# A two-block transformer on one core: norm roots kept 128 tokens wide, and modulation products packed whole between attention units

## The chip, the core and the metric

One core of a Trainium2 chip. The metric is the device time of one launch in microseconds, the median over the runs. All data and all matmuls are fp32. TensorE's clock is granted at one of two levels, 1.2 or 2.4 GHz; the profile shows it as 0.5 or 1.0 of full speed.

## What is computed

A sequence of 512 tokens of width 1024 passes two blocks. The first is a mixture of dilated causal attention (8 heads of 64), a short gated convolution and a cross-attention to 256 memory tokens, followed by an MLP of width 4096. The second adds latent attention and a gated linear recurrence (8 heads), both under a modulation by a condition vector, and a mixture of 32 experts (4 per token). Every part is framed by this norm:

```python
def rms_norm(x, g):
    y = x * lax.rsqrt(jnp.mean(x * x, axis=-1, keepdims=True) + EPS)
    return y * g
...
h = rms_norm(x, g_pre_mix);  proj = h @ w_in            # q, k, v, conv gates b, c, u, and qx
y_attn = dilated_mixture_attention(rope(q), rope(k), v)
y_conv = b * causal_conv3(c * u, conv_w)
y_x    = cross_attention(qx, rms_norm(mem, g_mem) @ w_mem_kv)
y = concat(rms_norm(y_attn), rms_norm(y_conv), rms_norm(y_x)) @ w_out
x = x + rms_norm(y);   x = x + rms_norm(relu(rms_norm(x) @ w_up)**2 @ w_down)
...
mod = silu([c, c_ctx]) @ w_mod + b_mod                  # 1024 x 6144, used from the second block on
```

## The kernel before

Activations lie feature-major: 128 features on the partitions, the 512 tokens (256 for memory and context) along the free dimension, so a 1024-wide row is eight chunks of 128x512. The five engines run their own instruction streams, written out by hand in one order each, and meet in semaphores.

**Weights.** `WT` (from `weight_tiles`, L69) lists all weight tiles of up to 1 MB in the order of use. SP loads them one after the other into a ring of five slots (L630 to L636): tile t waits until the last product pair that uses tile t-5 is complete (`s_pair`). A "pair" is a group of products that fills PSUM banks and is then evacuated by ScalarE (L1198). A w_mod set is a pair of its own kind (`quads`, L450 to L454): four tiles side by side, 32 products whose 32 stationary columns (the conditions) go to four column groups of the array and so to the four 32-partition strips of one bank, taken in turn (L779 to L789).

**First block.** After the pre_mix and mem norms the q, k, v products run (`in1`). Then come 48 attention units, each a head and a block of 128 queries: 32 of the dilated attention (`U_X` = 32, one to four key blocks) and 16 of the memory attention (two key blocks). In `attention` (L869) TensorE issues the scores of unit u+1, a first portion of side products, the transposes of the probabilities of u, a second portion, and the sum of values of u. VectorE does maxima and scaling, ScalarE exponentials and copies. So each unit has two slots for side products, and a list of weights per slot (`UNIT32`, `UNIT16`, `filled` L534) says how many products go where: the rest of w_in and the memory's keys and values (`side1`, 96 products) beside the dilated units, the six modulation sets (`mod`, 192 products, six in each slot) beside the memory units. Between the two runs of units VectorE does the convolution (L1551 to L1559). ScalarE follows the same lists to evacuate (L1227).

**Norms.** There are 23. `norm_stats` (L1454) squares a chunk on VectorE into one of two buffers `sq`; TensorE's `norm` (L823) multiplies it by a 128x128 matrix of ones, which sums over the partitions and repeats the sum on all 128 of them, and accumulates the chunks in `PT`. VectorE then scales and adds EPS (L1465), ScalarE takes the root (L1214), VectorE the reciprocal (L1467), all 128x512, and the chunks are multiplied by gain and `rstd` (`norm_apply` L1472, `add_normed` L1578, `modulated` L1601, `merge` L1642).

**Heads.** In the recurrence (L989 to L1041) the products of head n+1 fill 19 slots of head n (`HEAD_SLOTS`). At its end stand the last slot (`fill(18)`, eight products), the norm of the head's output, and the wait for the evacuation of the next head's products; then slot 0 of the next head with 26 products.

## Time and profile before

| | us |
|---|---|
| median of 3 runs (lowest to highest) | 3635.74 (3634.92 to 3641.96) |
| the profiled execution | 3640.03 |
| its span, first to last instruction | 3638.3 |
| TensorE busy, mean granted clock | 3082.0, 0.908 |
| VectorE busy / ScalarE busy | 1067.0 / 656.8 |
| first-block attention units (148 to 413 us) | 265.4 |
| expert stage (from about 2406 us) | some 1170 |

The rows further down come from the page of this execution and from views of its trace. In a table of stretches the columns are the stretch, its length, then busy time and number of instructions of TensorE (PE), its weight loads (PEld), VectorE (DVE), ScalarE (ACT) and GpSimd (POOL), the granted clock, and the share and rate of DMA. In a list in order of time the columns are start, duration (from first to last of the merged instructions), engine, line, operation, output and inputs with shapes, count, and in brackets how long the engine was idle before and what ended it. In the chain of waits they are start, length, what. Groups of instructions give count, busy time in all, and the mean of one in ns. An fp32 product appears as two MATMUL records.

### The profile page before, as it was taken

Reading aid. Unit: us, or ns where it says so; the run is one execution under the profiler, and the core shown is the slowest. Engines: PE = TensorE matmul, PEld = TensorE weight load, DVE = VectorE, ACT = ScalarE, POOL = GpSimd, SP = SyncE. Lnnn points to the kernel's source line nnn. Section 1 sums busy time; section 2 is a strip of 40 time slices with the busy share of each in tenths; the row PEclk is TensorE's granted clock in tenths of the full one; section 3 lists DMA queues with packets and bytes.
Section 4 is the critical chain, followed back from the end, with each engine's and each line's share of the span. In section 5 each row is a group of like instructions: output and inputs, shape, how many; then the busy total and the mean of one; then the engine's idle time right before and its main releaser. Section 6 shows DMA issues by size and latency. Waiting matters only on the chain.

```text
span 3638.3 us, 44181 instructions
## 1 busy us (share of the span) xinstructions
PE 3082.0 (85%) x18888; PEld 1555.5 (43%) x18888; DVE 1067.0 (29%) x1997; ACT 656.8 (18%) x1344; POOL 193.9 (5%) x180
## 2 busy tenths in 40 slices
PE   6896579999967999899999958458899999899873
PEld 3552234444423666566666644323333333333321
DVE  3342331000042221455555552511111111111115
ACT  1131100000000333344444430001111111011000
POOL 0000000000000000111111110100000000000001
PEclk9997799999988999999999968579999999899886
DMA  4113312212110011411111100347789899999993
GB/s 151 47 47 151 139 46 70 69 46 93 79 39 28 24 47 35 185 41 41 41 41 41 41 12 2 134 113 309 321 361 374 362 387 399 392 379 398 394 381 135
DMA packets 119321, 581.36 MB, mean 160 GB/s; under 512 B 12806, under 2 KB 24086, under 8 KB 72534
## 3 DMA queue, kind: packets, MB, share of 16 engines
q1 hardware_dynamic: 92274, 531.96, 37.2%
q10 hardware_dynamic: 20436, 24.26, 1.9%
q0 software_dynamic: 6416, 22.32, 1.8%
q8 instruction: 150, 2.46, 0.3%
q14 instruction: 45, 0.37, 0.0%
HBM read 550.02 MB, written 28.47 MB: 159 GB/s over the span
## 4 chain that ended last, share of the span: by engine, by line
PE 73%; DMA 13%; DVE 9%; ACT 2%; issue 1%; POOL 1%; ACTq 0%; SPq 0%; DVEq 0%; POOLq 0%
PE product_banks L798 36%; PE product_banks L1097 12%; DMA space<-in_wgu 10%; PE product_banks L1119 7%; PE score_banks L1026 3%; PE turn_bank L829 3%; DVE rstd L1467 1%; DMA space<-in_wt 1%; PE product_banks L785 1%; PE out_bank L905 1%; PE score_banks L844 1%; DMA y_rows<-zeros 1%; PE out_bank L866 1%; PE score_banks L886 1%; DVE space L1680 1%
## 5 line engine op out<-in xcount | busy, mean ns | idle before, releaser
L798 PE MATMUL product_banks<-space 128*128 128x512 f32 (+2 forms) x4016 | 1430.0, 508 | 56.7 <-DVE space L1602 15.3
L798 PEld LDWEIGHTS product_banks<-space 128*128 128x128 f32 x4016 | 706.7, 194 | 674.8 <-issue 584.4
L1097 PE MATMUL product_banks<-space 128*32 128x512 f32 x5440 | 660.3, 620 | 83.9 <-DMA space<-in_wgu 82.5
L1097 PEld LDWEIGHTS product_banks<-space 128*32 128x32 f32 x5440 | 158.4, 111 | 459.5 <-issue 299.4
L1119 PE MATMUL product_banks<-space,rstd 128*32 128x256 f32 x5440 | 329.5, 397 | 1.1 <-ACT rstd L1402 0.6
L1799 DVE TENSOR_TENSOR sq<-product_banks,space 128x512 f32<-128x512 f32 x85 | 58.8, 692 | 835.1 <-PE product_banks L1097 835.1
L1207 ACT ACTIVATE space<-product_banks 128x512 f32<-128x512 f32 (+1 forms) x234 | 114.1, 525 | 837.4 <-PE product_banks L798 834.4
L1119 PEld LDWEIGHTS product_banks<-space,rstd 128*32 128x32 f32 x5440 | 184.2, 116 | 176.8 <-issue 81.5
L829 PE MATMUL turn_bank<-sq,cst 128*128 128x512 f32 (+1 forms) x196 | 107.5, 688 | 112.1 <-DVE sq L1463 111.8
L712 POOL TENSOR_TENSOR space<-space 128x512 f32<-128x512 f32 x112 | 133.0, 1202 | 1034.1 <-ACT space L1341 941.4
L1026 PE MATMUL score_banks<-space 128*128 128x64 f32 x896 | 132.2, 300 | 28.0 <-issue 21.1
L1463 DVE TENSOR_TENSOR sq<-space 128x512 f32<-128x512 f32 (+1 forms) x58 | 34.4, 607 | 384.0 <-PE turn_bank L829 281.1
L1026 PEld LDWEIGHTS score_banks<-space 128*128 128x128 f32 x896 | 129.0, 221 | 36.9 <-issue 32.5
L1398 ACT ACTIVATE ms<-sq 128x256 f32<-128x256 f32 x85 | 35.4, 416 | 478.2 <-DVE sq L1802 478.2
L829 PEld LDWEIGHTS turn_bank<-sq,cst 128*128 128x128 f32 x196 | 39.5, 230 | 175.6 <-DVE sq L1463 140.7
L1402 ACT ACTIVATE rstd<-turn_bank 128x256 f32<-128x256 f32 x85 | 32.6, 384 | 384.1 <-PE turn_bank L1108 384.1
L785 PE MATMUL product_banks<-space,conditions 128*32 128x256 f32 x384 | 57.0, 506 | 36.5 <-DMA space<-in_wt 36.5
L1086 PE MATMUL score_banks<-cst,space 128*128 128x128 f32 x176 | 25.1, 289 | 66.8 <-DMA space<-h_rows,space 66.8
L1586 DVE TENSOR_TENSOR space<-space 128x1024 f32<-128x1024 f32 x16 | 19.6, 1225 | 200.9 <-ACT space L1207 200.9
L1467 DVE RECIPROCAL rstd<-ms 128x512 f32<-128x512 f32 (+1 forms) x23 | 72.3, 3144 | 21.1 <-ACT ms L1214 21.1
L1701 DVE COPY_PREDICATED space<-cst,score_banks 128x256 f32<-128x256 uint8 x112 | 58.3, 520 | 57.9 <-PE score_banks L1026 57.3
L1813 DVE TENSOR_TENSOR zeros<-product_banks,space 128x256 f32<-128x256 f32 x85 | 36.1, 424 | 132.5 <-PE product_banks L1119 125.8
(259 smaller groups left out, 2334.1 us busy)
## 6 DMA issues: line engine op xcount, KB each, us to landing
space<-in_wgu SPq DMA_DIRECT2D x256, 1024.0 KB, 15.4
space<-in_wdn SPq DMA_DIRECT2D x128, 1024.0 KB, 22.6
space<-in_wt SPq DMA_DIRECT2D x104, 1024.0 KB, 5.0
y_rows<-zeros ACTq DMA_DIRECT2D x2, 6400.0 KB, 28.7
y_rows<-zeros ACTq DMA_DIRECT2D x85, 128.0 KB
space<-in_wt SPq DMA_DIRECT2D x13, 512.0 KB, 4.3
space<-in_wt SPq DMA_DIRECT2D x4, 768.0 KB, 4.2
x<-in_xT SPq DMA_DIRECT2D x1, 2048.0 KB, 15.6
```

What stands on the lines that cost most here:

```text
L712: gp.tensor_tensor(dlt[:, L % 2, 0:T].rearrange("p (b s) -> p b s", s=2 * hf), c3, ref.broadcast_to([P, nb, 2 * hf]), ALU.subtract).then_i ...
L785: ins = nc.tensor.matmul(bank[row:row + rows, 0:cols], lhsT, rhs, start=(i == 0), stop=(i == DC - 1))
L798: ins = nc.tensor.matmul(bank[0:rows, at:at + cols], lhsT, rhs, start=(i == 0), stop=(i == len(mm) - 1))
L829: nc.tensor.matmul(PT[:, 0:w], ones, sq[:, g % 2, 0:w], start=(c == 0), stop=(c == nch - 1)).then_inc(s_mm, 1)
L844: ins = nc.tensor.matmul(S[:, a:b], l, r, start=(i == 0), stop=(i == len(grp) - 1))
L1026: ins = nc.tensor.matmul(LB[L % 2][:, 64 * c:64 * c + 64], X[:, L % 2, cs_], half, start=True, stop=True)
L1097: ins = nc.tensor.matmul(bank[ROWS * g:ROWS * g + ROWS, :], xT_[:, k, :], w[:, 512 * g:512 * g + 512], start=(k == 0), stop=(k == DC - 1))
L1119: ins = nc.tensor.matmul(bank[ROWS * g:ROWS * g + ROWS, :], aT_[:, P * c + ROWS * d:P * c + ROWS * d + ROWS], w[:, c, 256 * g:256 * g + 25 ...
L1207: ins = nc.scalar.activation(dst, src, func, bias=bias, scale=scale)
L1467: link(V.reciprocal(rstd[:, 0:w], ms[:, 0:w]))
L1701: V.copy_predicated(to, mk, LB[L % 2][:, 0:256].rearrange("p (c b s) -> p c b s", c=TT, s=hf)).then_inc(s_at, 1)
L1799: V.tensor_tensor(tbuf, bank, bias[:, 0:512], ALU.add).then_inc(s_u, 1)
```

## The change

Two parts, both in the order of the instruction streams.

1. **Norms.** The sum of a chunk becomes four products with 32 columns of ones, one for each block of 128 tokens (64 for the 256-token norms), written to the four 32-partition strips of `PT`. The sum of token 128q+i then lies in strip q, column i, and the tile is 128x128 and not 128x512. ScalarE takes the root straight from PSUM, with scale and EPS inside the same instruction (EPS is a new constant column), VectorE the reciprocal of 128x128. TensorE then spreads it (`norm_spread`): four products with one identity column, repeated 128 times, as the stationary operand, which write 128x512 into `PO`. The applications read `PO` in place of `rstd`. VectorE's scaling step is gone; TensorE has a new wait for the reciprocal (`s_inv`), VectorE one for the spread (`s_rs`). In the heads the spread of head n-1 stands in head n, behind three products of the filler (`lead`).
2. **Side products.** Both runs of units become one, with one list of 96 slots, `SIDE_SLOTS`: qx, km, vm with two products a slot in units 0 to 11; then each modulation set whole (32 products) in one slot, at slots 27, 41, 55, 69, 80 and 91 (unit = slot / 2), and behind the first three a w_in tile (cc, cu, cb) over twelve slots with 2, 1, 1 products in turn; all other slots are empty. The tiles are loaded in the new order. The convolution's two halves stand in VectorE's stream behind units 36 and 40.

```diff
@@ weight_tiles
-    for i in range(10):
+    for i in range(6):
         cols("w_in", 256 * i, 256)
+    cols("w_in", 256 * 9, 256)
     for i in range(2):
         cols("w_mem_kv", 256 * i, 256)
-    for i in range(24):
-        cols("w_mod_2", 256 * i, 256)
+    for i in range(6):
+        for j in range(4):
+            cols("w_mod_2", 256 * (4 * i + j), 256)
+        if i < 3:
+            cols("w_in", 256 * (7, 8, 6)[i], 256)
...
-        UNIT16, UNIT32 = [1] * 32, [1] * 64
+        SET, ONE = 4 * DC, [2, 1, 1] * 4
+        SIDE_SLOTS = ([2] * 24 + [0] * 3 + [SET] + ONE + [0, SET] + ONE + [0, SET] + ONE + [0, SET]
+                      + [0] * 10 + [SET] + [0] * 10 + [SET] + [0] * 4)
...
+                def lead(self, n):
+                    for _ in range(n):
+                        next(self.steps)
+                    self.done += n
...
-                    nc.tensor.matmul(PT[:, 0:w], ones, sq[:, g % 2, 0:w], start=(c == 0), stop=(c == nch - 1)).then_inc(s_mm, 1)
+                    for q in range(4):
+                        ins = nc.tensor.matmul(PT[ROWS * q:ROWS * q + ROWS, 0:w // 4], ones[:, 0:ROWS], sq[:, g % 2, w // 4 * q:w // 4 * (q + 1)],
+                                               start=(c == 0), stop=(c == nch - 1))
+                    ins.then_inc(s_mm, 1)
+
+            def norm_spread(name):
+
+                n = NI[name]
+                w = NORMS[n][3]
+                pe.wait_ge(s_inv, n + 1)
+                for q in range(4):
+                    ins = nc.tensor.matmul(PO[:, w // 4 * q:w // 4 * (q + 1)], ident[:, ROWS * q:ROWS * q + 1].broadcast_to([P, P]),
+                                           rstd[:, 0:w // 4], start=True, stop=True)
+                ins.then_inc(s_rs, 1)
...
             norm("pre_mix")
+            norm_spread("pre_mix")
             norm("mem")
+            norm_spread("mem")
...
-            attention(0, U_X, Filler("side1", UNIT32))
-            pe.wait_ge(s_evac, stages["side1"][1])
             pe.wait_ge(s_silu, 1)
-            attention(U_X, U_M, Filler("mod", UNIT16))
-
-            pe.wait_ge(s_evac, stages["mod"][1])
+            attention(0, U_M, Filler("side", SIDE_SLOTS))
+
+            pe.wait_ge(s_evac, stages["side"][1])
...
+                    if n and d == 0:
+                        if filler:
+                            filler.lead(3)
+                        norm_spread(f"head{n - 1}")
                     fill(2 * d)
...
-                w = NORMS[n][3]
-                act.wait_ge(s_ms, n + 1)
-                nc.scalar.activation(ms[:, 0:w], ms[:, 0:w], F.Sqrt).then_inc(s_rt, 1)
+                _, _, nch, w = NORMS[n]
+                act.wait_ge(s_mm, chunk0[n] + nch)
+                nc.scalar.activation(ms[:, 0:w // 4], PT[:, 0:w // 4], F.Sqrt, bias=const("eps"), scale=1.0 / (P * nch)).then_inc(s_rt, 1)
...
-                dve.wait_ge(s_mm, chunk0[n] + nch)
-                V.tensor_scalar(ms[:, 0:w], PT[:, 0:w], 1.0 / (P * nch), EPS, ALU.mult, ALU.add).then_inc(s_ms, 1)
                 dve.wait_ge(s_rt, n + 1)
-                link(V.reciprocal(rstd[:, 0:w], ms[:, 0:w]))
+                V.reciprocal(rstd[:, 0:w // 4], ms[:, 0:w // 4]).then_inc(s_inv, 1)
+                dve.wait_ge(s_rs, n + 1)
...
-                    V.scalar_tensor_tensor(dst[:, c, 0:w], src[:, c, 0:w], gain(c), rstd[:, 0:w], ALU.mult,
+                    V.scalar_tensor_tensor(dst[:, c, 0:w], src[:, c, 0:w], gain(c), PO[:, 0:w], ALU.mult,
                                            ALU.mult).then_inc(s_norm, 1)
...
+            def between(u):
+                if u == U_X + 4:
+                    dve.wait_ge(s_evac, conv_end)
+                if u in (U_X + 4, U_X + 8):
+                    convolve(u // (U_X + 8))
+
+            attention(0, U_M, between)
```

## Rows read from the trace of the kernel before

**Rows 1.** The page: busy time of the engines; the chain that ended last, by engine.
```profile
PE 3082.0 (85%) x18888; PEld 1555.5 (43%) x18888; DVE 1067.0 (29%) x1997; ACT 656.8 (18%) x1344; POOL 193.9 (5%) x180
PE 73%; DMA 13%; DVE 9%; ACT 2%; issue 1%; POOL 1%; ACTq 0%; SPq 0%; DVEq 0%; POOLq 0%
```
**Rows 2.** Table of stretches: the 48 attention units.
```profile
148.00:413.40 265.40, 218.85 (x1009) 110.97 (x1009) 77.86 (x234) 66.14 (x211) 0.00 (x0) 0.84 0.27 104
```
**Rows 3.** Tables of stretches inside the attention units.
```profile
183.40:200.75 17.35, 17.35 (x64) 9.18 (x63) 6.72 (x20) 5.98 (x18) 0.00 (x0) 1.00 0.04 5
249.73:262.33 12.60, 12.59 (x64) 8.98 (x63) 6.62 (x21) 5.34 (x16) 0.00 (x0) 1.00 0.02 6
279.90:288.00 8.10, 0.70 (x3) 0.29 (x2) 7.08 (x13) 0.84 (x3) 0.00 (x0) 0.67 0.38 129
295.87:299.48 3.61, 3.61 (x34) 1.80 (x33) 1.09 (x4) 1.11 (x4) 0.00 (x0) 1.00 0.00 0
300.10:413.40 113.30, 76.36 (x427) 31.40 (x425) 13.65 (x50) 16.83 (x60) 0.00 (x0) 0.70 0.47 186
```
**Rows 4.** The chain of waits: first and last of five waits for sets' weights.
```profile
300.99 9.01 DMA space<-in_wt
...
392.04 8.88 DMA space<-in_wt
```
**Rows 5.** In order of time: the pre_mlp norm.
```profile
531.14 1.29 DVE L1463 TENSOR_TENSOR sq<-x 128x512 f32<-128x512 f32 x2
...
541.31 0.69 DVE L1465 TENSOR_SCALAR ms<-turn_bank 128x512 f32<-128x512 f32 x1 [1.22 <-PE turn_bank L829]
542.03 0.63 ACT L1214 ACTIVATE ms<-ms 128x512 f32<-128x512 f32 x1 [26.41 <-DVE ms L1465]
542.70 3.35 DVE L1467 RECIPROCAL rstd<-ms 128x512 f32<-128x512 f32 x1 [0.69 <-ACT ms L1214]
546.08 4.07 DVE L1472 SCALAR_TENSOR_TENSOR space<-x,vec,rstd 128x512 f32<-128x512 f32 x6
```
**Rows 6.** The chain of waits: a down group of the expert stage, at full clock.
```profile
2421.49 3.45 PE product_banks L1119 x64
```
**Rows 7.** Groups of instructions by shape.
```profile
L1224 ACT ACTIVATE space<-score_banks,small 128x256 f32<-128x256 f32 x16 | 7.5, 469 | 7.1 <-DVE small L1500 7.1
...
L1243 ACT ACTIVATE space<-out_bank 64x128 f32<-64x128 f32 x48 | 13.1, 272 | 75.3 <-PE out_bank L866 74.7
...
L1467 DVE RECIPROCAL rstd<-ms 128x256 f32<-128x256 f32 x3 | 5.3, 1754 | 1.4 <-ACT ms L1214 1.4
...
L1495 DVE SCALAR_TENSOR_TENSOR space<-score_banks,cst 128x512 f32<-128x512 f32 x8 | 5.5, 692 | 9.0 <-PE score_banks L844 9.0
...
L1472 DVE SCALAR_TENSOR_TENSOR space<-x,vec,rstd 128x512 f32<-128x512 f32 x24 | 16.2, 747 | 0.1
```
**Rows 8.** Table of stretches: the rope products ahead of the units.
```profile
132.00:139.00 7.00, 3.38 (x6) 0.89 (x6) 6.46 (x10) 0.00 (x0) 0.00 (x0) 1.00 0.01 5
```
**Rows 9.** The chain of waits: from one head to the next, and one 128-column product.
```profile
1564.07 1.09 ACT space L1207 x2
...
1565.20 22.58 PE product_banks L798 x52
...
1644.12 0.22 PE score_banks L1028 x2
```
**Rows 10.** In order of time: the post_mix norm, behind products that end at 506.57.
```profile
506.41 7.82 PE L829 MATMUL turn_bank<-sq,cst 128*128 128x512 f32 x16
...
519.04 0.75 DVE L1578 SCALAR_TENSOR_TENSOR space<-space,vec,rstd 128x512 f32<-128x512 f32 x1
```
**Rows 11.** In order of time: the conv norm, first squares and first applications.
```profile
427.97 1.28 DVE L1463 TENSOR_TENSOR sq<-space 128x512 f32<-128x512 f32 x2
...
437.31 1.41 DVE L1472 SCALAR_TENSOR_TENSOR space<-space,vec,rstd 128x512 f32<-128x512 f32 x2
```
**Rows 12.** In order of time: VectorE's decayed keys in head 1.
```profile
1585.39 0.95 DVE L1673 TENSOR_TENSOR space<-space 128x768 f32<-128x768 f32 x1
```

60 lines of the change are left out of this document (40 added, 20 removed).

## The prediction

> **What bounds the kernel now.** I read the page first [rows 1]: TensorE is busy for 85% of the span and makes 73% of the chain that ended last, DMA another 13%. Most of that DMA is the expert stage at the end, which the change doesn't touch: it only starts earlier or later. So each stage ahead of it counts with its full length. The table by stage comes next [rows 2]: the 48 attention units of the first block take 265.4 us, with TensorE busy for 218.9 and its granted clock at 0.84 on the mean. Inside it [rows 3]: four units beside twelve 512-wide side products take 17.35 us with TensorE never idle; beside twelve 256-wide ones 12.60 us; then 8.1 us in which VectorE does the convolution and TensorE 0.7 us of work; then 113.3 us of memory units with the modulation sets, TensorE busy 76.4 and the clock at 0.70. The chain says why: five times it waits about 9 us for weights [rows 4]. A set uses four tiles at once, the ring has five slots, and all four come free at the set's last product, so three of the next four tiles can't be asked for before that.
>
> The norms are the second place. In the pre_mlp norm [rows 5] the reader sees two squares done in 1.29 us but all eight summed only 10.1 us after the first began: the sums go at TensorE's pace, not at VectorE's. Then a chain of wide operations in which TensorE does nothing: scaling 0.69, root 0.63, reciprocal 3.35 us, 4.8 us from the last sum to the first application. That chain is on the path in the 15 norms outside the heads; in the first six heads it is covered.
>
> **The attention stage.** The queue of tiles decides the gain. A set now runs whole (32 products) in one slot, and three of the six sets have a w_in tile with 16 products behind them, spread over six units. The tiles of the next set are asked for at the end of a set, and land while those units run: six units of about 4 us against 9 to 12 us for four tiles. Behind the fourth and fifth set stand five units without side work, at 2.4 us each 12 us, against 9 us [rows 4]: just covered, 0 to 2 us may show. So I cost the weights at nothing in five places; what covers them are those units, and if they were faster than 1.8 us each, the wait would come back. SP's queue keeps the order in which the tiles are used, and nothing else is issued from it here.
>
> What a set costs: 32 products of 256 columns by four column groups. The down products of the expert stage are the same form, 64 instructions for 32 products in 3.45 us at full clock [rows 6]. So a set is 3.45 us, 6.9 at the half clock. In six-product portions a unit with two portions took 3.61 us [rows 3], of which the portions are about 2.0; 32 products in portions thus cost 5.3 us.
>
> Units: 17.35 less twelve products of 0.86 leaves 7.1 us for four attention units on TensorE. Then:
> - units 0 to 3, today 18.0 us with a cold start, now with 16 products in place of 12: 22.5;
> - units 4 to 11 with 4 products of 256 columns each: 2 x (7.2 + 6.9) = 28.2;
> - units 12 and 13, no side work but one set: 2.2 + 5.0 = 7.2;
> - units 14 to 33 with 48 products (41.3), 18 attention units (32.9), two memory units (3.2) and two sets (6.9): 84.3;
> - units 34 to 47, memory units alone with three sets and the two halves of the convolution. A unit without side work isn't shown before; TensorE's part of it is 1.6 us (3.61 less the portions) and its chain of exponential (0.47 [rows 7]), sum read, reciprocal, scaling, transposes, copy is longer. Between 1.6 and 3.6 I take 2.4, since each step but the portions stays. 14 x 2.4 + 3 x 3.0 + 2.5 for the half of the convolution that no set covers = 45 at full clock, 63 at half clock; I take 50.
>
> The sum is 192 us against 265.4: **73 us less**, 53 to 80 with the ends of the last term and of the weights. The 8.1 us stop for the convolution goes with it: its first half (five operations) now stands behind the maxima of unit 37, its second beside the fifth set; what waits behind it on VectorE is the scaling of the next unit's probabilities, and TensorE's transposes wait for that.
>
> The clock is the open side of the last term. With TensorE busy for 3.4 of 7.0 us the clock stayed at 1.00 for that stretch [rows 8] and fell soon after; in the 113 us with waits its mean is 0.70 [rows 3].
>
> **The norms.** The end of one, from the last sum on: the root of 128 columns out of PSUM 0.28 (a 64x128 copy out of PSUM takes 0.272 [rows 7]); the reciprocal, by 3.353 us for 512 and 1.754 for 256 columns [rows 5, 7] 6.2 ns a column over 0.15, so 0.95 for 128; four products of 128 columns at 0.22 each [rows 9] and the way out 0.2, so 1.1 us at full clock and 2.1 at half; handovers 0.2. That is 2.5 us at full and 3.5 at half clock for 4.8: 2.3 or 1.3 us less. The sums: four narrow products in four column groups are 0.22 to 0.43 us for 0.86 (the lower end by four-way overlap, the upper by the 54 ns an instruction of rows 6), so VectorE's squares set the pace, 0.69 each, or 0.98 where the half clock and the two buffers hold it back. Eight chunks from a standstill: 10.1 us now [rows 5], 5.7 to 8.3 then, 7.2 taken.
> - pre_mlp, mix2, ffn2, final (from a standstill, half clock): about 4.5 each, 18.
> - post_mix and post_mlp (behind products, 12.5 us from the last product to the first application [rows 10]): squares 2 to 7 are left, 2.8 off the sums and 1.8 off the end, 9.2.
> - attn 2.9, conv and xattn 3.5 each (9.3 us from the first square to the application now [rows 11], 5.8 then): 9.9.
> - ctx 1.9, qin 3.8, ckv_lat 3.5; at ckv_ctx the rope product stands behind the new spread in TensorE's queue, and the products after it start at half clock where they were at full: 0 and -1.5. Sum 7.7.
> - pre_mix 4, but the mem norm gets a new wait: TensorE must spread its root before the first products (3 us), though they never needed it, and starts them at the half clock: 1 in all, between -2 and 5.
> - heads 0 to 5: here TensorE is the path. The sum costs nothing before and after: it lies beside ScalarE's 1.09 us evacuation [rows 9]. VectorE comes to its decayed keys at 1586.34 and TensorE at 1587.79 [rows 9, 12], so VectorE's saved 1.6 us buy nothing, and the spread adds 0.9 us to TensorE: 6 x 0.9 = 5.4 more. The new wait for the reciprocal stands behind three led products (2.6 us), and by the table load and root on ScalarE the reciprocal ends at just about that time: 0, or 0.3 each. Behind that wait are the 23 other products of the slot. Heads 6 and 7 are bound by VectorE: 1.5 and 2.4 less. Sum -1.5.
>
> All norms: 18 + 9.2 + 9.9 + 7.7 + 1 - 1.5 = **44 us less**, 30 to 55.
>
> The application now reads its root out of PSUM. An operation of that kind takes 0.692 us for 512 columns with a PSUM operand and 0.747 with all in SBUF [rows 7], so I cost it at nothing. The Trainium skill (VectorE: DVE Perf Modes, section "The TRN2 errata") charges VectorE 120 fixed cycles for a PSUM source where SBUF costs 58; over 98 applications that would be an estimated 6 us more. The trace disagrees for this form.
>
> **The sum.** 73 + 44 = 117. The profiled execution took 3640.0 us (span 3638.3, 1.7 around it); less 117 that is 3523. The median of the runs lies 4.3 us under it, so I forecast 3519.
>
> **Rivals.** A: the last units run slow. Once TensorE has gaps the clock drops, the sets there cost 6.9 us each, and the weights of sets five and six show as well. For it speaks the 0.70 of the stretch with waits, against it rows 8. The stage then takes 212 us, the gain is 53 + 44 less some 10 for products that start cold: about 3549. The Trainium skill (TensorE: Matmul & The Clock Gate, section "HAM oscillation") has the gate fall back in loops whose matmuls wait in between; by that rule this is the case. The trace agrees that gaps bring the half clock, not that gaps this short do.
> B: the norms give little. The sparse sums keep the clock low, each spread costs 2.1 us or more, and the stages behind start cold for longer; also the wait in the heads is real (the reciprocal as late as today, 1570.5, makes 2.7 us a head). The norms then give 10 and not 44: 3553.
> C, the slower one: TensorE's new wait in the heads. It holds back the whole filler of the slot, which the end of the stage needs. To eat 117 us it would need 17 us in each of seven heads; the latest time that a row supports is those 2.7. It decides only if VectorE's reciprocal waited for work behind TensorE's wait: 3660.
> D: the change does less than it says, the narrow products not overlapping: four times 0.21 is what one wide one takes now, so only the sums' 20 us are lost: 3539. Inside the range.
>
> **How the numbers follow.** Forecast with D (3496 to 3545) 0.75; A 0.11; B 0.08; a larger gain, under 3496, 0.03; C 0.03. The range 3496 to 3556 holds the first three. A measurement of this kernel tells about 0.2% (7 us) from no change; faster by more 0.96, within 0.01, slower 0.03.
>
> **What would show it.** No wait for weights over 2 us in the attention stage, a set of 64 instructions in about 3.5 us, the stage near 192 us; if it is over 210, look at the granted clock behind unit 34. In a norm, first square to first application in about 11 us for eight chunks where it was 15; a reciprocal of 0.95; the applications still 0.75, or the PSUM price was wrong. In the heads a period 0.9 us longer; if TensorE sits idle ahead of a spread there, the led products were too few. I would be wrong most likely in units 34 to 47 and in how long the half clock lasts behind each norm.

## The result and the profile after

The changed kernel takes 3527.6 us (median of four runs, 3524.8 to 3533.7) against 3638.7 us for the kernel before: a ratio of 0.970, with a 95% interval of 0.968 to 0.972. Forecast were 3519 us, in a range of 3496 to 3556. Its profiled execution took 3530.2 us with a span of 3528.5, against 3640.0 and 3638.3; the two spans differ by 109.8 us, which the table of stages below divides up.

The page of the changed kernel, busy time of the engines, the granted clock in 40 slices, and the chain that ended last, by engine:

```profile
PE 3039.7 (86%) x19660; PEld 1568.9 (44%) x19660; DVE 994.3 (28%) x1974; ACT 651.0 (18%) x1344; POOL 194.1 (6%) x180
...
PEclk9998889999889999999999958599999999999886
...
PE 74%; DMA 12%; DVE 9%; ACT 2%; issue 2%; POOL 1%; ACTq 0%; SPq 0%; DVEq 0%; POOLq 0%
```

Against [rows 1]: TensorE makes 772 more instructions, for the column groups and spreads, and is still the engine of the chain; VectorE is relieved of 73 us, of which only what stood on the path could show.

The attention units of the changed kernel, by stretch (units 0 to 3, 4 to 11, 12 and 13, 14 to 33, 34 to 47; time, length, then busy time of PE, PEld, DVE, ACT and POOL with their instructions, the granted clock, the DMA share and GB/s); the last line is the sum:

```profile
144.50:169.75 25.25, 23.82 (x73) 11.96 (x73) 7.91 (x25) 6.01 (x19) 0.00 (x0) 0.86 0.00 1
169.75:198.05 28.30, 28.30 (x142) 21.01 (x141) 13.46 (x40) 11.28 (x37) 0.00 (x0) 1.00 0.22 75
198.05:205.97 7.92, 6.85 (x78) 3.72 (x77) 3.37 (x10) 2.90 (x9) 0.00 (x0) 1.00 0.40 134
205.97:290.91 84.94, 84.93 (x418) 45.12 (x417) 32.16 (x97) 28.02 (x87) 0.00 (x0) 1.00 0.45 174
290.91:346.20 55.29, 45.35 (x303) 25.21 (x302) 20.95 (x63) 17.23 (x61) 0.00 (x0) 0.72 0.51 199
sum 201.70, PE 189.26 PEld 107.02 DVE 77.85 ACT 65.43 POOL 0.00; mean PE 37.85 PEld 21.40 DVE 15.57 ACT 13.09 POOL 0.00
```

That is 201.7 us where [rows 2] had 265.4: 63.7 less. From 170 to 291 us the clock is 1.00 and TensorE idles only 1.1 us, in the units 12 and 13; the units 34 to 47, in the last line, idle 9.9 us and have the clock at 0.72. The waits for weights of [rows 4] are gone. The sets in order of time, the first and the last three:

```profile
201.74 3.66 PE L796 MATMUL product_banks<-space,conditions 128*32 128x256 f32 x64
...
291.91 3.66 PE L796 MATMUL product_banks<-space,conditions 128*32 128x256 f32 x64
314.37 5.77 PE L796 MATMUL product_banks<-space,conditions 128*32 128x256 f32 x64
335.50 5.45 PE L796 MATMUL product_banks<-space,conditions 128*32 128x256 f32 x64
```

A set is 3.66 us for its 64 instructions at full clock (3.45 by [rows 6]) and 5.5 to 5.8 where part of it falls into the half clock.

The pre_mlp norm of the changed kernel, in order of time, from its first squares to its application; it answers to [rows 5]:

```profile
450.89 1.29 DVE L1510 TENSOR_TENSOR sq<-x 128x512 f32<-128x512 f32 x2
451.64 1.25 PE L846 MATMUL turn_bank<-sq,cst 128*32 128x128 f32 x16 [12.85 <-DVE sq L1510]
...
457.37 0.37 ACT L1262 ACTIVATE ms<-turn_bank,cst 128x128 f32<-128x128 f32 x1 [21.70 <-PE turn_bank L846]
457.77 0.95 DVE L1512 RECIPROCAL rstd<-ms 128x128 f32<-128x128 f32 x1 [1.17 <-ACT ms L1262]
458.77 2.08 PE L856 MATMUL out_bank<-rstd,cst 128*128 128x128 f32 x8 [1.48 <-DVE rstd L1512]
460.89 5.36 DVE L1518 SCALAR_TENSOR_TENSOR space<-x,vec,out_bank 128x512 f32<-128x512 f32 x8 [2.17 <-PE out_bank L856]
```

From the first square to the first application it is 10.0 us where it was 14.9. The sums now come in 1.25 us for two chunks (sixteen instructions) and VectorE's squares set the pace; from the root's start to the application it is 3.5 us, of which the spread at the half clock is 2.1. The eight applications read PSUM and take 5.36 us, one every 0.67 us, against 0.68 in [rows 5]: no slower than before.

By stage, the two traces laid side by side:

| stage | before, us | after, us | less |
|---|---|---|---|
| ahead of the first scores | 148.0 | 144.5 | 3.5 |
| the 48 units | 265.4 | 201.7 | 63.7 |
| modulation; attn, conv and xattn norms | 36.0 | 27.05 | 9.0 |
| post_mix and pre_mlp norms | 40.3 | 31.5 | 8.8 |
| post_mlp and mix2 norms | 42.3 | 32.5 | 9.8 |
| ctx, qin and ckv norms, up to the latent attention | 123.7 | 113.5 | 10.2 |
| six periods of the heads, from the end of head 0 | 552.95 | 562.8 | 9.8 *more* |
| the last two norms of heads, up to the next products | 99.5 | 96.5 | 3.1 |
| from there to the first expert (ffn2 norm) | 196.4 | 189.4 | 7.0 |
| the final norm | 27.7 | 21.8 | 5.9 |

The stages with nothing changed in them, taken together, are 1.5 us slower; two of them (the MLP's products, and the latent attention with what follows up to the end of head 0) take some 1 us more each.

### The profile page after: what moved, and what is told of

It reads as the page before. It is cut to its first block, busy times and chain, and to the rows that moved or that the text cites. A ratio compares the mean times of both kernels' runs of the same rounds, so it can differ in the third digit from the quotient of the medians.

```text
span 3528.5 us, 45703 instructions
## 1 busy us (share of the span) xinstructions
PE 3039.7 (86%) x19660; PEld 1568.9 (44%) x19660; DVE 994.3 (28%) x1974; ACT 651.0 (18%) x1344; POOL 194.1 (6%) x180
## 4 chain that ended last, share of the span: by engine, by line
PE 74%; DMA 12%; DVE 9%; ACT 2%; issue 2%; POOL 1%; ACTq 0%; SPq 0%; DVEq 0%; POOLq 0%
PE product_banks L809 37%; PE product_banks L1144 13%; DMA space<-in_wgu 10%; PE product_banks L1166 7%; PE score_banks L1071 3%; PE out_bank L936 1%; PE out_bank L856 1%; PE score_banks L873 1%; DMA y_rows<-zeros 1%; PE out_bank L895 1%; DVE sq L1510 1%; PE turn_bank L846 1%; PE product_banks L796 1%; PE score_banks L917 1%; DVE space L1731 1%
## 5 line engine op out<-in xcount | busy, mean ns | idle before, releaser
L1071 PEld LDWEIGHTS score_banks<-space 128*128 128x128 f32 x896 | 130.4, 223 | 36.9 <-issue 32.5
L846 PE MATMUL turn_bank<-sq,cst 128*32 128x128 f32 (+1 forms) x784 | 49.1, 348 | 88.8 <-DVE sq L1510 88.7
L745 POOL DMA_INDIRECT space<-h_rows,space x22 | 20.9, 952 | 971.4 <-PE score_banks L1133 948.3
L846 PEld LDWEIGHTS turn_bank<-sq,cst 128*32 128x32 f32 x784 | 18.1, 126 | 124.0 <-DVE sq L1510 94.6
L1760 DVE TENSOR_TENSOR space<-space 128x256 f32<-128x256 f32 x112 | 69.2, 618 | 12.8 <-ACT space L1405 12.8
```

Source lines behind the costliest of these rows:

```text
L846: ins = nc.tensor.matmul(PT[ROWS * q:ROWS * q + ROWS, 0:w // 4], ones[:, 0:ROWS], sq[:, g % 2, w // 4 * q:w // 4 * (q + 1)], start=(c == 0 ...
L1071: ins = nc.tensor.matmul(LB[L % 2][:, 64 * c:64 * c + 64], X[:, L % 2, cs_], half, start=True, stop=True)
L1760: V.tensor_tensor(xv[:, :, qh], ev[:, :, qh], views(qq, hf)[:, :, qh], ALU.mult)
```

## Experiments

Every edit is one to the changed kernel unless it says the kernel before. Each run was timed beside the kernel before on the same chip, whose medians lay at 3637.0 to 3638.4 us; the changed kernel's own 3527.6 us is the yardstick for edits to it.

**1. The two parts alone.** The first kernel is the kernel before with all the norm hunks of the diff (constant, semaphores, `norm`, `norm_spread`, `norm_root`, `norm_stats`, the applications, the head's lead) and none of the others; the second has the others alone.

> The kernel before with the norm part alone: four column groups, narrow root, spread, the head's lead of three products; the tile order and the side products of the kernel before. The theory of two separate parts: between the two traces the stretches outside the attention stage add up to 46 us less, and the attention stage to 64 us less, and neither needs the other, so this kernel takes 3638.7 - 46 = 3593 us (3587 to 3599), with its attention stage of 48 units still at 265 us and its heads still 10 us longer over six of them. The rival: the parts need each other (the norms' gain is lent by what stands before them, or the first units' clock hangs on it), and this kernel comes out above 3603 or under 3583.

> The kernel before with the side part alone: the new tile order, one list of slots, whole sets, the convolution between two units; the norms of the kernel before. By two separate parts: 3638.7 - 64 = 3575 us (3569 to 3581), the attention stage 202 us. By the rival (the parts need each other) it is outside 3565 to 3585.

Measured: norms alone 3590.1 us (ratio 0.988, 0.986 to 0.990), 47.3 us less than the kernel before; side part alone 3571.2 us (0.983, 0.981 to 0.984), 66.2 less. Together 113.5, where both at once gave 111.1. Both lie in the ranges of the theory of two separate parts: what one part lends the other is less than the runs tell apart, some 9 us, and the prediction's two sums can be judged each by itself. The profiled executions are no good for this addition. The one of the side part lies 7.5 us under its median, with an attention stage of 194.9 us and not 202, and the one of the norms 6 us under its median, with a stage of 261.5 us and six head periods 7.0 us longer and not 10. Experiments 2 and 6 show that the granted clock moves both stages by that much.

The side part itself has three ingredients (the order of the tiles, the whole sets, the place of the convolution). Experiment 4 takes away the second; the first and the third were not run alone.

**2. The heads with the wide norm.** In heads 0 to 5 sums, step, root and reciprocal go back to 512 columns; the spread and the lead are left out there:

```diff
+                    if name in WIDE:
+                        nc.tensor.matmul(PT[:, 0:w], ones, sq[:, g % 2, 0:w], start=(c == 0), stop=(c == nch - 1)).then_inc(s_mm, 1)
+                        continue
...
-                    if n and d == 0:
+                    if n and d == 0 and f"head{n - 1}" not in WIDE:
```

> The changed kernel, but the norms of heads 0 to 5 as before: one sum product of 512 columns, a VectorE step on 512, a root and a reciprocal of 512, nothing spread and no lead. Theory A, the narrow norm costs time there, since TensorE's chain sets the head's end while VectorE has slack: the periods of heads 0 to 5 go back from 93.8 to 92.2 us on average and the kernel takes 3527.6 - 9.8 = 3518 us (3514 to 3521). Theory B, the ten microseconds lie in something else that the two traces differ in there (stretches at the lower clock that came by chance, the weights' transfers): within 3 us of the changed kernel, 3525 to 3531.

Measured: 3518.7 us (ratio 0.968, 0.966 to 0.970), 9.0 us faster than the changed kernel, each of its four executions under each of the changed kernel's. The narrow norm costs time there. The applications in its six heads, by line:

```profile
L1711 DVE SCALAR_TENSOR_TENSOR space<-space,vec,rstd x6: 750/752/753, 1467.3 to 1927.9; 128x512 f32<-128x512 f32 x6
```

Five periods from the first to the sixth make 92.1 us each, where the changed kernel's six make 93.8. Where the difference arises is seen by laying one head of each trace side by side: the last slot, the sum of the norm, the next products. First the changed kernel, then this one:

```profile
1549.67 7.03 PE L809 MATMUL product_banks<-space 128*128 128x512 f32 x16
1556.63 0.43 PE L846 MATMUL turn_bank<-sq,cst 128*32 128x128 f32 x8
1557.87 2.84 PE L809 MATMUL product_banks<-space 128*128 128x512 f32 x6 [0.82 <-ACT space L1255]
```

```profile
1545.57 7.03 PE L814 MATMUL product_banks<-space 128*128 128x512 f32 x16
1552.44 1.02 PE L851 MATMUL turn_bank<-sq,cst 128*128 128x512 f32 x2
1553.77 22.58 PE L814 MATMUL product_banks<-space 128*128 128x512 f32 x52 [0.32 <-ACT space L1263]
```

The narrow sum is done in 0.43 us and not 1.02, and TensorE then waits 0.82 and not 0.32 us for ScalarE's evacuation: from the start of the slot to the next products it is 8.20 us in both, and in the kernel before. The shorter sum buys nothing there and costs nothing. From those products to the next scores it is 23.41 us against 22.42: that is the spread, 0.99 us in each head, 5.9 in six. The other 3.9 of the 9.8 us by which the changed kernel's six periods are longer than those before lie in one later stretch, which begins with the first products of 64 columns, behind some 3.5 us in which TensorE stands still. It holds the same instructions in every head. The longest of the changed kernel's, and the one of the same head here:

```profile
1509.99:1544.12 34.13, 34.13 (x216) 30.31 (x217) 18.30 (x41) 9.52 (x26) 10.95 (x10) 0.85 0.01 1
```

```profile
1509.05:1540.02 30.97, 30.97 (x216) 27.15 (x217) 20.22 (x41) 9.53 (x26) 11.22 (x10) 0.94 0.00 1
```

TensorE is busy throughout both; the half clock lasts longer in the first. The stretch takes 31.0 us in three of the changed kernel's six heads and 32.3, 32.4 and 34.1 in the others, against 31.0 or 31.7 in the kernel before. So theory A holds for the spread, and theory B (stretches at the lower clock) for the rest. With the norm part alone this second share was 1.1 us and not 3.9; why the clock comes back later in some heads is not shown.

**3. The lead taken away.**

```diff
-                        if filler:
-                            filler.lead(3)
                         norm_spread(f"head{n - 1}")
```

> The changed kernel without the three products that run ahead of the wait for the inverse root in heads 1 to 6. In the trace of the changed kernel these three take 1464.75 - 1461.90 = 2.84 us and the spread starts right behind them, 0.98 us after the reciprocal's start at 1463.57. Theory A, TensorE's chain sets the head, and the three products then come behind the wait: 6 heads by 1.2 to 2.8 us, 3527.6 + 7 to 17 = 3535 to 3545 us. Theory B, VectorE's decayed keys are as late as TensorE there, so that the products find another gap: within 4 us of the changed kernel. The third case of my prediction, a stall of 17 us a head, is looked for in the same place: it would be over 3600 us.

Measured: 3552.7 us (ratio 0.977, 0.975 to 0.979), 25.1 us over the changed kernel, 4.2 us a head, more than theory A's upper end. In order of time, TensorE at the end of head 1 and VectorE's reciprocal; first the changed kernel, then this one:

```profile
1556.63 0.43 PE L846 MATMUL turn_bank<-sq,cst 128*32 128x128 f32 x8
...
1557.87 2.84 PE L809 MATMUL product_banks<-space 128*128 128x512 f32 x6 [0.82 <-ACT space L1255]
...
1559.54 0.95 DVE L1512 RECIPROCAL rstd<-ms 128x128 f32<-128x128 f32 x1 [8.34 <-ACT ms L1262]
...
1560.55 1.15 PE L856 MATMUL out_bank<-rstd,cst 128*128 128x128 f32 x8
```

```profile
1558.77 0.43 PE L846 MATMUL turn_bank<-sq,cst 128*32 128x128 f32 x8
...
1561.67 0.95 DVE L1510 RECIPROCAL rstd<-ms 128x128 f32<-128x128 f32 x1 [8.34 <-ACT ms L1260]
...
1562.77 1.13 PE L856 MATMUL out_bank<-rstd,cst 128*128 128x128 f32 x8 [3.58 <-DVE rstd L1510]
```

I had priced the wait by the length of the three products; it is the length of the chain that they cover, sum to reciprocal's end, with 1.28 us of a table load on ScalarE in it: 3.58 us of standing TensorE. In the changed kernel TensorE stands for 0.82 us at this place too, for the evacuation, so the stop grows by 2.76 us a head, 16.6 in six. The six periods of this trace are 19.9 us longer. The difference is the clock: in three of the six heads it is at the lower level behind the stop (23.9 to 24.0 us for products that take 22.3 in the others, and in two of the three a spread of 2.0 us where it is 1.1), and in the later stretch of experiment 2 it came back sooner than in the changed kernel, 2.7 us in all. What makes up the remaining 5 us of the 25.1 is not shown; executions differ by as much. The new wait in the heads, rival C's place, is real and costs 3 to 4 us a head where nothing covers it; the 17 us that the rival needed aren't there.

**4. What "whole" is worth.** The tile order stays, the sets and the convolution's products are dealt out evenly; in the second kernel a set runs in two halves in one unit:

```diff
-        SIDE_SLOTS = ([2] * 24 + [0] * 3 + [SET] + ONE + [0, SET] + ONE + [0, SET] + ONE + [0, SET]
-                      + [0] * 10 + [SET] + [0] * 10 + [SET] + [0] * 4)
+        SIDE_SLOTS = [2] * 24 + [3, 3, 4] * 24
```

```diff
+        SIDE_SLOTS = ([2] * 24 + [0] * 2 + [16, 16] + ONE + [16, 16] + ONE + [16, 16] + ONE + [16, 16]
+                      + [0] * 9 + [16, 16] + [0] * 9 + [16, 16] + [0] * 4)
```

> The changed kernel with its tile order, but the 240 products of the modulation sets and of the convolution's three parts dealt evenly, 3, 3 and 4 to a slot, over slots 24 to 95. Theory A, the order of the tiles did it (the weights for the sets are asked for over 200 us and not over 113) and that a set runs whole gives nothing: this kernel takes what the changed one takes, 3524 to 3532 us, or less, since the last 14 units are then filled evenly: down to 3517. Theory B, whole sets are worth something of their own, since four column groups need to follow one another closely and each portion makes a unit's chain longer: 3538 us or more (48 units at 0.2 us or more each), the stage over 212 us where it is 201.7 us.

> The changed kernel, but each modulation set runs in two halves of 16 products, in the two slots of one unit (before its transposes, and between them and its value products) instead of whole in the second of them. The dealt-out set of the run before it cost 31 us. Theory A, what counts is how long a set holds its four slots of the ring: a half set more ahead of it holds them some 2 us longer, nothing against the 20 to 30 us between sets, so this kernel is within 4 us of the changed one, 3520 to 3532, on the quicker side if the first half fills TensorE's wait for the probabilities (up to 0.7 us a set). Theory B, any portion costs, since four column groups run close only in a long row: every further portion 0.5 us or more, and 3533 us or more.

Measured: dealt out 3558.5 us (ratio 0.979, 0.977 to 0.981), 31 us slower; in halves 3531.7 us (0.971, 0.969 to 0.973), 4 us over the changed kernel, which the runs don't tell apart, at the upper edge of theory A. My first theory (the order of the tiles did it all) fell, though not for all of the gain: dealt out, the kernel with the new order and the moved convolution is still 32 us faster than the norm part alone. Dealing out also makes more portions, so theory B as I wrote it, that each costs, was met in the total; but the halves show that one portion more in each set costs little, by the medians 0.7 us a set. The trace of the dealt-out kernel names what it is: the waits for weights are back. Two stretches of its late units, and TensorE's waits over all of them:

```profile
292.00:320.00 28.00, 24.82 (x129) 10.99 (x128) 10.29 (x31) 8.57 (x29) 0.00 (x0) 0.87 0.26 92
320.00:346.00 26.00, 18.85 (x102) 7.99 (x102) 8.15 (x23) 5.10 (x18) 0.00 (x0) 0.75 0.35 137
```

```profile
PE product_banks L795 <- DMA space<-in_wt: 13.2, 6, 4.9
```

The changed kernel moves 185 and 217 GB/s in about these stretches (292 to 320 and 320 to 346 us), this one 92 and 137. A set occupies four of the ring's five slots until its last product. Dealt over some ten slots it holds them for five units, and only then can the next three tiles be asked for; run whole, it holds them for 3.7 us, and the units between two sets are time for the transfers. SP's queue shows it: from 190 us to the end of the stage it waits 114.2 us for the slots of sets in the dealt-out kernel and 64.4 in the changed one, six times each. The waits are 13.2 of the 27 us by which its stage is longer (144.8 to 373.7 us); the remaining 14 lie in smaller portions and a clock of 0.87 from 197 us on, which no run tells apart.

**5. The first products ahead of the memory norm.**

```diff
-            norm("mem")
-            norm_spread("mem")
             pe.wait_ge(s_norm, normed("pre_mix", 1))
-            products("in1", "pre_mix")
+            for i, _ in enumerate(product_steps("in1")):
+                if i < DC - 1:
+                    pe.wait_ge(s_norm, normed("pre_mix", i + 2))
+                if i == 15:
+                    norm("mem")
+                if i == 31:
+                    norm_spread("mem")
```

> The changed kernel, but the first products start as soon as the first chunk of the first norm is written; the memory norm's sums stand behind the first 16 products and its spread behind 32, and ScalarE empties the first pair of banks before its sines. My prediction put the memory norm's new wait ahead of the first products at only 1 us. The trace of the changed kernel has the first chunk of the norm at 28.6 us and the first products at 40.19 us. Theory A, TensorE's products are all that the first 145 us wait for: the kernel gains 11.5 us less the spread and the sums that now stand between products (2 to 3 us), 3527.6 - 9 = 3519 us (3516 to 3522). Theory B, VectorE's angle and rotation work or the weights are next in line: within 4 us of the changed kernel, 3524 to 3531.

Measured: 3524.0 us (ratio 0.969, 0.967 to 0.971), 3.7 us less, at the edge of what the runs tell apart and, by its time, where theory B put it; the trace is clearer. The first products in the changed kernel, and the first products, the sums' start and the spread in this one:

```profile
40.19 18.40 PE L809 MATMUL product_banks<-space 128*128 128x512 f32 x40
```

```profile
28.49 16.10 PE L809 MATMUL product_banks<-space 128*128 128x512 f32 x32 [0.84 <-DVE space L1523]
...
44.52 0.43 PE L846 MATMUL turn_bank<-sq,cst 128*32 128x64 f32 x16
...
47.70 14.00 PE L809 MATMUL product_banks<-space 128*128 128x512 f32 x32
...
61.54 1.00 PE L856 MATMUL out_bank<-rstd,cst 128*128 128x64 f32 x8
```

The products start 11.7 us earlier and the first scores come 6.3 us earlier (144.5 to 138.2 us): the first sixteen products follow the norm's chunks and take 2.1 us longer than the next sixteen, and 3.2 + 0.8 us of sums and spread now stand between products. So TensorE's products are what the first scores wait for, as in theory A, but I had allowed too little for what moves in between them. The edit takes away more than the new wait: the sums of the memory norm stood ahead of the first products in the kernel before too (they started at 45.20 us there).

**6. The last units and the clock.** Three kernels: the convolution behind all units; its ten operations one behind each of the units 36 to 45; and that with a product nobody reads in each empty slot from unit 34 on:

```diff
-            attention(0, U_M, between)
+            attention(0, U_M)
+            dve.wait_ge(s_evac, conv_end)
+            convolve(0)
+            convolve(1)
```

```diff
+            def between(u):
+                k = u - (U_X + 4)
+                if k == 0:
+                    dve.wait_ge(s_evac, conv_end)
+                if 0 <= k < 10:
+                    convolve(k // 5, k % 5)
```

```diff
+                    def idle(i):
+                        if u >= U_X + 2 and SIDE_SLOTS[i] == 0:
+                            nc.tensor.matmul(S[:, 512:768], ident, cst[:, 0:256], start=True, stop=True)
```

> The changed kernel, but both halves of the convolution run behind all 48 units instead of between two of them each. In the trace of the changed kernel TensorE idles 2.47 us over the first half at 301.3 to 303.8 us, and from there to 314 us every product takes the time of the lower clock. Theory A, that stop is what took the clock down: the units behind it run at 2.24 us instead of 3.53, and the stage ends 346.2 - 2.5 - 5 to 7 us, at about 337 to 339, while the convolution's 2 x 3.4 us now stand on VectorE ahead of the norms: the kernel takes within 4 us of the changed one. Theory B, the clock falls in these thinly filled units anyway: the stage ends at 343 to 346 us and the kernel takes 3 to 7 us more, 3530 to 3535.

> The changed kernel, but the convolution's ten VectorE operations run one behind each of the units 36 to 45 instead of five behind unit 36 and five behind unit 40. With the convolution behind all units the clock stayed at 1.00 to 314 us instead of falling at 304, and the attention stage ended at 339.0 instead of 346.2 us, but its 6.8 us then stood in front of the norms. Theory A, single operations of at most 0.75 us fit into VectorE's pauses within a unit: stage end at 338 to 341 us and 3527.6 - 6 = 3522 us (3519 to 3525). Theory B, each lengthens its unit's chain by its own length, 10 x 0.67: the stage ends at 345 us or later and the time is that of the changed kernel, 3525 to 3531.

> As the split convolution, and in the units 34 to 47 each slot without a side product gets one product of 128 by 256 columns whose result nobody reads (nothing is left out). A unit without side work takes 2.24 us at the full clock and 3.53 us at half, and TensorE idles about half of it. Theory A, the granted clock falls in these units because TensorE is thinly filled there, and filling brings it back: clock 0.95 or more from 289 us to the end of the stage, stage end at 332 to 336 us, 3517 us (3513 to 3520), 5 us under the split convolution alone. Theory B, the clock falls for another reason, and the 24 added products of 0.43 us (0.86 at half clock) only cost: the stage ends 5 to 12 us later than with the split convolution alone.

Measured: convolution last 3528.4 us (ratio 0.971, 0.969 to 0.973), as the changed kernel; split 3524.5 us (0.970, 0.968 to 0.971; single executions from 3513 to 3530); filled 0.969 (0.966 to 0.971), three executions at 3517.9, 3519.6 and 3528.7 us, and a fourth that took 7979 us, more than twice the others, whose cause is not known and which is left out. None of the three is told apart from the changed kernel by its interval, and the split convolution lies between its two theories. The stretches of the traces say more. The changed kernel, then the convolution last, then split, then filled:

```profile
303.00:314.00 11.00, 8.51 (x24) 5.15 (x24) 3.87 (x15) 3.34 (x12) 0.00 (x0) 0.50 0.38 160
```

```profile
304.00:314.00 10.00, 8.34 (x87) 4.97 (x88) 2.97 (x13) 3.68 (x13) 0.00 (x0) 1.00 0.46 168
...
320.00:339.00 19.00, 16.05 (x101) 8.63 (x100) 6.43 (x20) 5.58 (x20) 0.00 (x0) 0.67 0.39 152
```

```profile
304.00:314.00 10.00, 8.31 (x88) 4.89 (x88) 4.92 (x15) 3.69 (x13) 0.00 (x0) 1.00 0.44 163
...
320.00:339.00 19.00, 13.09 (x139) 7.79 (x138) 9.09 (x32) 6.32 (x18) 0.00 (x0) 1.00 0.74 296
```

```profile
293.00:340.00 47.00, 44.97 (x355) 27.92 (x353) 20.35 (x63) 17.29 (x61) 0.00 (x0) 1.00 0.62 239
```

With the convolution in one block between two units TensorE stands for 2.5 us, and in each of the six such traces taken (the changed kernel, the side part alone, the wide heads, the halves, the early products, no lead) the clock is down to its lower level behind it. With the convolution last it stays up through there, the stage ends at 339.0 us as theory A had it, and the clock falls later, at 315 us, in units with nothing in TensorE's way but their own chain. With it split, the trace shows the full clock to the end of the stage, at 332.2 us; but the other three executions took 10 to 17 us more than the profiled one, and what their clock was can't be seen. So at this place the fall goes with the stop: six traces of six with it, none of two without.

The stop is not needed for a fall, though. The changed kernel's clock comes back within the fifth set and falls a second time at 325.6 us, behind two units in which TensorE never idled over 0.6 us at once:

```profile
320.07:325.56 5.49, 3.79 (x23) 2.27 (x19) 2.19 (x8) 3.09 (x11) 0.00 (x0) 1.00 0.80 291
325.56:335.50 9.94, 8.81 (x24) 5.11 (x24) 3.18 (x12) 2.81 (x11) 0.00 (x0) 0.50 0.63 264
```

The wide heads, the halves, the early products and no lead show the same second fall, between 319 and 329 us. With the one of the convolution last that is a fall in thin units alone in six of the eight traces without filling; the side part alone and the split convolution have none. In the changed kernel the two falls cost about the same: three units at about 3.5 and not 2.24 us and some 2 us in the set behind them, 6.0 us for the first and 5.4 for the second, and 2.5 for the stop itself. Together that is the difference between its stage of 201.7 us and the 187.6 us of the split convolution's trace. What decides whether thin units lose the clock is not shown.

Filled, both traces that have it (this and the combination below) show 1.00 to the end, and a unit then takes 2.72 us where an empty one takes 2.24 at full clock and 3.53 at half: the stage takes 194.2 us (145.8 to 340.0), 7.5 less than in the changed kernel and 6.6 more than with the split convolution where that kept the clock. Theory A was right about the clock and theory B about the price. Two traces don't show that filling keeps the clock each time: one execution of the filled kernel took 9 us more than the other two.

**7. Narrow, or only one hop fewer?** The kernel before, with ScalarE's root taken straight from the sums' bank and nothing else changed:

```diff
-                act.wait_ge(s_ms, n + 1)
-                nc.scalar.activation(ms[:, 0:w], ms[:, 0:w], F.Sqrt).then_inc(s_rt, 1)
+                act.wait_ge(s_mm, chunk0[n] + nch)
+                nc.scalar.activation(ms[:, 0:w], PT[:, 0:w], F.Sqrt, bias=const("eps"), scale=1.0 / (P * nch)).then_inc(s_rt, 1)
...
-                dve.wait_ge(s_mm, chunk0[n] + nch)
-                V.tensor_scalar(ms[:, 0:w], PT[:, 0:w], 1.0 / (P * nch), EPS, ALU.mult, ALU.add).then_inc(s_ms, 1)
```

> The kernel before, but ScalarE takes the root straight from the sums' bank, with the scale and the small constant in its instruction; sums, root and reciprocal keep their 512 columns and nothing is spread. It tells what of the norm part is the narrow width and what is the removed VectorE step. By the rows of the kernel before, the step takes 0.69 us and stands on the path in the 15 norms outside the heads and in the last head or two: 3638.4 - 11 = 3627 us (3622 to 3631). If the removed hop is worth more than the step's own time, under 3620 us; if the root from the bank is slower than from memory by as much, 3633 to 3640 us.

Measured: 3630.5 us (ratio 0.998, 0.997 to 0.999), 6.6 us less, with the interval from 3 to 10. The norm part gives 47, and 54 to 56 without its loss in the heads, so by difference some 7 of it are the hop and the rest is width: sums at VectorE's pace and a short reciprocal, less the spread. The wide root by its line:

```profile
L1214 ACT ACTIVATE ms<-turn_bank,cst x23: 474/687/688, 28.8 to 3613.5; 128x512 f32<-128x512 f32 x20, 128x256 f32<-128x256 f32 x3
```

It takes 0.687 us from PSUM with scale and constant, 0.629 from SBUF in the kernel before: the hop's 0.69 is gone for 0.06.

**8. Together.** Wide norms in heads 0 to 5, early first products, the convolution split and the last units filled:

> Four edits of the changed kernel together: the wide norm in heads 0 to 5 (-9), the first products ahead of the memory norm (-4 to -6), the convolution in single operations (-6) and the filled last units (-5, or a loss of 5 to 12 if filling doesn't hold the clock). If they add up: 3527.6 - 25 = 3503 us (3498 to 3508); if the filling costs, 3510 to 3522 us.

Measured: 3503.4 us (3501.9 to 3506.4; ratio 0.963, 0.962 to 0.965), 24 us under the changed kernel, in the range for "they add up", and the fastest of all; its four executions lie within 4.5 us. What the runs showed of the parts alone adds up to 21 (9.0, 3.7, and 8 for the split convolution filled, by the median of its three executions). Its 48 units end at 331.5 us and take 193.4:

```profile
289.00:331.50 42.50, 40.47 (x299) 25.21 (x287) 18.97 (x58) 15.50 (x55) 0.00 (x0) 1.00 0.61 241
```

## Why the prediction came out as it did

The forecast lay 9 us under the measured median. Between the two profiled executions 7 are missing; the rest is my base, since with a fourth run the kernel before has a median of 3638.7 and not 3635.7 us. By the sums the 7 lie in the attention stage: 63.7 us less instead of 73, norms and what follows them 46 instead of 44. That the second sum came so close is partly luck: the heads gave 5 us less than forecast, and the first norms, ctx to ckv, ffn2 and final gave 9 more.

- **Weights at nothing in five places**: right. No wait for weights stands in the stage, and TensorE is busy throughout the units 4 to 11 and 14 to 33. The cover that I named, four to six units between two sets, is what the dealt-out kernel took away, and 13 us of waits came back.
- **Units 4 to 11 and 14 to 33**, 28.2 and 84.3 forecast: 28.3 and 84.9. Units 12 and 13, 7.2: 7.9. The term "so many products by the time of one, plus TensorE's own part of the units" holds to 1% where TensorE is never idle.
- **Units 0 to 3**, 22.5 forecast: 25.25. The step that failed is the base, "today 18.0 us": I cut the kernel before one unit too early. By the same boundary it had 22.6, and the four products more make the 2.7. (18.0 and four products of 0.86 would even have been 21.4; the further 1.1 in my 22.5 stands in no row.)
- **Units 34 to 47**, 50 forecast between 45 and 63: 55.3. Here I had weighed the clock and taken a third of the way; it was nearer six tenths. The unit without side work is 2.24 us at full clock (2.4 taken), but the clock fell at 304 us, came back, and fell again at 325.6, and six of the fourteen units took about 3.5. Rival A's mechanism is therefore real, at its place, though the weights that it wanted to add didn't show: its price was 5 us and not 30. [Rows 8] misled me: there the clock stood through 7 us of half-idle TensorE; here one fall came behind 2.5 us of standing still and one behind thin units alone.
- **A set**: 3.45 forecast, 3.66 measured, 5.5 to 5.8 where 6.9 was feared, since the clock comes back within it.
- **The end of a norm**, 2.5 or 3.5 us: 3.5 at half clock as said; the reciprocal's 0.95 exact, the root 0.37 and not 0.28. The spread was at half clock even in post_mix, right behind products, so that norm gave 8.8 with pre_mlp and not 9.1. The eight sums took 6.4 us, from the first square to the last sum, of the 7.2 allowed.
- **Norms from a standstill**, 4.5 each (my own terms, 2.9 off the sums and 1.3 off the end, give 4.2): 4.9 in pre_mlp by itself; ffn2 with what is around it 7.0, final 5.9. **Attn, conv, xattn**, 9.9: 9.0. **Ctx to ckv**, 7.7: 10.2 with the query products in it. All a little off, nothing fell.
- **The first norms**, 1 us, between -2 and 5: 3.5, inside. The wait that I charged there is real: from the end of the memory norm's sums to the first products it is 2.8 us in the changed kernel (37.4 to 40.2), 3 forecast. Moving it, with the sums, behind the first products gave 6 us at the first scores.
- **The heads**, 1.5 more forecast: 6.8 more. This is the mis-sized term of the norm part. What I counted was right: the sum costs nothing before and after, the wait is covered, and the spread is 0.99 us a head for the 0.9 taken, 5.9 in six for 5.4. Left out, at nothing, was that the half clock later in the head can last longer: 3.9 us in this trace, 1.1 with the norm part alone. So six heads cost 9.8; heads 6 and 7 gave 3.1 instead of 3.9. The three led products were enough, just: the spread starts 0.06 us behind the reciprocal's end.
- **The PSUM operand at nothing**: right. An application takes 0.747 us from PSUM in the heads against 0.752 from SBUF in the wide ones. The estimate from the Trainium skill (VectorE: DVE Perf Modes, section "The TRN2 errata") would have added 6 us; this form doesn't show it.
- **Rival B** (10 from the norms) fell with the norms alone at 47 us less; **D** fell with the sums: two chunks' eight products in 1.25 us, where one behind the other, at the 0.22 us of [rows 9], they would take 1.8 even at full clock.

## What to carry to other kernels

Time a transfer not only by when its data are wanted but by how long their predecessors hold their slots: work that uses many slots at once should run in one go, with other work behind it while they refill; the same products in the same order, dealt out evenly, cost 31 us. Before a shortened chain is put everywhere, ask in each place which engine is the path: where TensorE was, the narrow norm that saves 5 us elsewhere cost the 1.0 us of its spread, and 1.6 with what the clock added. And a wait moved onto the busiest engine is free only if the work led ahead of it is as long as the whole chain it waits for, table loads included.

## What the runs showed of the chip that I had not expected

- The granted clock fell to its lower level behind a stop of TensorE of 2.5 us among half-idle units in six traces of six, and stayed up at that place in two of two without the stop. In six of the eight traces it also fell in such units with no stop over 0.6 us ahead of it; in two it did not. The last 14 units are worth up to 14 us one way or the other (41 us in the trace that kept the clock, 55 in the changed kernel's), and a program's executions can differ by that: 3513 to 3530 us with the split convolution. The Trainium skill (TensorE: Matmul & The Clock Gate, section "HAM oscillation") describes loops with waits in between that fall back; the traces agree, but show that the same units can also run through at full clock, and that waits of 0.6 us each were enough in six of eight.
- With a product of 128 by 256 columns in each idle slot the clock was 1.00 in both traces that have it, and each such unit paid 0.48 us for it; the split convolution alone had 1.00 in its one trace too, so this is not shown to be the filling's doing.
- The root by ScalarE straight from PSUM, with a scale and a constant per partition, costs 0.06 us over the plain one from SBUF at 512 columns.
